# Moving one tile's transposes into the first tile's matmuls, and four weight splits to earlier page pairs, in a 2-layer decoder kernel

## The chip, the cores and the metric

The kernel is one program on one core of a Trainium2 chip. Its time is the device time of one execution in microseconds (us), and the number given for a kernel is the median of several executions. TensorE (PE in the profile) does the matmuls; VectorE (DVE), ScalarE (ACT) and GpSimd (POOL) do the rest of the arithmetic; SyncE (SP) issues every DMA. Each engine works through its own instructions in the order in which the program has them, and the engines meet only at semaphores: one engine waits until a counter that another one raises has reached a value.

## What is computed

Two layers of a decoder step on 512 prompt tokens and 8 sequences of 8 new tokens. Cut from the reference:

```python
def layer_forward(x, pos, p, ret_s0, ret_chunk, attend):
    h = rmsnorm(x, p['norm_w'])
    z = h @ p['w_in']                       # 1024 x 3264, all branches at once
    ...
    o_r, s_new = retention_scan(q_r, k_r, v_r, ret_s0.astype(jnp.float32), ret_chunk)
    ...
    o_a = attend(qn, qp, c, kpe, p).reshape(b, t, MLA_WIDTH) * jax.nn.silu(g_a)
    y = jnp.concatenate([o_r, o_a], axis=-1) @ p['w_out']   # 1024 x 1024
    return x + y, c, kpe, s_new.astype(x.dtype)
```

For the new tokens, `attend` reads 16 cached pages of 128 keys for each of the 8 sequences, projects the cached latents to keys, and attends over them.

## The kernel before, in words

Each layer L has three stages. **Stage 0** is the input projection. The tokens stand in five tiles t (four of 128 prompt rows, one of 64 sample rows). A tile is normed on DVE (`norm(t)`, L1588), turned by 8 transposes on PE (`x_turn(t)`, L593; 4 of them to a bank of PSUM, the memory that matmuls write), and kept as two parts, a high one by ACT (`keep_x_hi`, L1157) and a low one by DVE (`keep_x_lo`, L1574). A product of full precision is three matmuls: high by high, low weight by high, high weight by low (L562, L563, L564). The 3264 weight columns come in 8 groups g of 408; each group has four pieces `raw` of 2 chunks of the contraction each, split into `w_hi` (ACT, L1186) and `w_lo` (DVE, L1596). `tile_product(g, t)` is then 8 chunks c by 3 matmuls. In group 0 and tile 0 the products wait chunk by chunk for the weights (`w0`).

**Stage 1** is retention and the prompt's attention. **Stage 2** is decode, and then the output projection. Decode goes sequence by sequence, each in 8 pairs q of pages (`sequence`). For a pair, PE turns the next pair's latents (`turn_pair(n + 1)`, L954), then makes this pair's keys (`pair_keys`, 24 matmuls twice over one line, L977) and rotary scores (`pair_rotary`, L986). ACT keeps the turned latents (`keep_pair`, `cT_hi`, L1473, and `kpT`, L1476) and then squares this pair's keys (`square_pair`, L1486, L1489, L1491). DVE keeps the low part of the latents (`cT_lo`, L1983) and sums the squares (`sum_pair`, L2000). All three do the next pair's keeping ahead of this pair's squares and sums. The turned latents share one PSUM bank, so PE may only turn pair n + 1 once DVE has counted pair n's `cT_lo` (`c_lo_ok`).

Four pieces of the output weights (`wout0`, 344 columns) are loaded by SP at the beginning of stage 2 (L506), behind the 32 page loads of sequence 0 and ahead of those of sequence 1 (L490, L492). ACT and DVE split them into `w0_hi` (L1514) and `w0_lo` (L2064), one piece behind each of four pairs of the layer's first sequence. ACT's first piece waits for all four loads:

```python
                    if k == 0 and g == 0:
                        act.wait_ge(wout0_in, 16 * 4 * (L + 1))
```

The output projection, which reads them, comes after all eight sequences.

Of the kernel before, what the change touches and what calls it, by code (L numbers as in the profile page):

```python
# [39 lines left out]
DC = D // P  # L40
# [10 lines left out]
GW = COLS // NG  # L51
# [13 lines left out]
def rows(t):  # L65
    return ST if t == S_TILE else P
# [50 lines left out]
def build(nc, x_prompt, x_sample, cache_ckv, cache_kpe, state_ret, page_table, norm_w, w_in, q_a_norm_w,  # L117
# [57 lines left out]
    w_hi, w_lo = [], []  # L175
# [114 lines left out]
    ps = nc.alloc_psum_tensor("ps", [P, 8, 512], FP32)  # L290
# [4 lines left out]
    def sem(name, per_layer=True):  # L295
        s = nc.alloc_semaphore(name)
        if per_layer:
            layer_sems.append(s)
        return s
# [6 lines left out]
    BANK = (1, 2, 3, 4, 6)  # L306
# [6 lines left out]
    N_W = 4 * (NG + 3)  # L313
    N_RAW = NG + 1
    N_Y = 2 * TILES
    N_PAIR = NB * PAIRS
    W_PAR = (None, 1, 0)

    def mix_tile(k):
        return S_TILE if k == 0 else k - 1  # L320
# [14 lines left out]
    w_hi_ok, w_lo_ok, z_in_psum, z_kept = (sem(n) for n in  # L335
        ("w_hi_ready", "w_lo_ready", "z_in_psum", "z_kept"))
# [56 lines left out]
    def zc(t, c0, n):  # L393
        return z[0:rows(t), t, c0:c0 + n]
# [163 lines left out]
    def _(pe):  # L558
        def product(out, lhs, rhs, first, last):

            (a_hi, a_lo), (b_hi, b_lo) = lhs, rhs
            pe.matmul(out, a_hi, b_hi, start=first, stop=False)  # L562
            pe.matmul(out, a_hi, b_lo, start=False, stop=False)  # L563
            return pe.matmul(out, a_lo, b_hi, start=False, stop=last)  # L564

        def tile_products(out, t, w_h, w_l, chunks=range(DC), w0=None):

            for c in chunks:
                if w0 is not None and c % 2 == 0:
                    pe.wait_ge(w_lo_ok, w0 + c // 2 + 1)  # L570
                if t == S_TILE:
                    pe.matmul(out, hT_s[:, c, :], w_h(c), start=c == 0, stop=False)  # L572
                    m = pe.matmul(out, hT_s[:, c, :], w_l(c), start=False, stop=c == DC - 1)  # L573
                else:
                    rows_t = slice(t * P, (t + 1) * P)
                    m = product(out, (hT_hi[:, c, rows_t], hT_lo[:, c, rows_t]), (w_h(c), w_l(c)), c == 0, c == DC - 1)
            return m
# [3 lines left out]
        for L in range(DEPTH):  # L581

            def x_turn(t):

                n = rows(t)
                pe.wait_ge(x_normed, t + 1)
                for half in range(2):
                    u = 2 * t + half
                    if u >= 3:

                        pe.wait_ge(x_lo, u - 2)
                    for c in range(4):
                        m = pe.transpose(ps[:, X_BANKS[u % 3], c * P:c * P + n], zc(t, H0 + (4 * half + c) * P, P),  # L593
                                         ident[0:n, 0:n])
                    m.then_inc(x_turned, 1)

            def tile_product(g, t):
                if g == 0:
                    pe.wait_ge(x_lo, 2 * (t + 1))
                else:  # L600

                    pe.wait_ge(z_kept, (g - 1) * TILES + t + 1)
                w = (g + L) % 2
                tile_products(ps[:, BANK[t], 0:GW], t, lambda c: w_hi[w][:, c, :], lambda c: w_lo[w][:, c, :],
                              w0=N_W * L if g == 0 and t == 0 else None).then_inc(z_in_psum, 1)

            if L == 0:
                x_turn(0)
            x_turn(1)
            for t in range(TILES):  # L610
                if t >= 1 and t + 1 < TILES:
                    x_turn(t + 1)
# [455 lines left out]
            def out_chunks(g, t, chunks):  # L1068
# [3 lines left out]
                else:  # L1072
                    w_h, w_l = w_hi[W_PAR[g]], w_lo[W_PAR[g]]
                return tile_products(ps[:, BANK[t], 0:n_cols], t, lambda c: w_h[:, c, 0:n_cols],
# [75 lines left out]
    def _(act):  # L1150
# [11 lines left out]
        for L in range(DEPTH):  # L1162
# [303 lines left out]
            def keep_pair(n, q, first):  # L1466

                par = q % 2
                act.wait_ge(c_turned, n + 1)
                if not first:  # L1470

                    act.wait_ge(rp_ps, n - 1)
                act.activation(cT_hi[:, par, :, :].rearrange("p a n -> p (a n)"), ps[:, 0, :], ACT.Copy)\  # L1473
                    .then_inc(c_hi_ok, 1)
                act.wait_ge(kp_turned, n + 1)
                act.activation(kpT[:, par, :], ps[:, 5, 0:P], ACT.Copy).then_inc(kpT_ok, 1)  # L1476
# [17 lines left out]
            def tail_exp(s, b):  # L1494
                act.wait_ge(sh_ok, s + 1)
                act.activation(Pr[:, b, :, :], Ssc[:, b, :, :], ACT.Exp).then_inc(pr_ok, 1)

            def split_out(g, chunks=range(4)):
                n = OG[g + 1] - OG[g]
                for k in chunks:  # L1500
                    if k == 0 and g == 0:
                        act.wait_ge(wout0_in, 16 * 4 * (L + 1))
                    if k == 0 and g == 1:

                        act.wait_ge(wout1_in, 16 * 4 * (L + 1))
                        act.wait_ge(ds_ok, 2 * NB * (L + 1))
                    if g == 2:
                        if k == 0:

                            act.wait_ge(dy_ps, L + 1)  # L1510
                        act.wait_ge(raw_in[k], 16 * (N_RAW * L + NG + 1))
                    src = (wout0[:, k, :, :], wout1[:, k, :, :], raw[:, k, :, 0:n])[g]
                    dst = w0_hi if g == 0 else w_hi[W_PAR[g]]
                    act.activation(dst[:, 2 * k:2 * k + 2, 0:n], src, ACT.Copy).then_inc(w_hi_ok, 1)  # L1514
# [8 lines left out]
            def keep_y_hi(t):  # L1523
                keep_hi(t, Y_BANKS, y_turned, N_Y * L, y_hi, 0.5)

            def sequence(seq, b, first, last):
                for q in range(PAIRS):
                    n = seq * PAIRS + q
                    if q + 1 < PAIRS or not last:
                        keep_pair(n + 1, (q + 1) % PAIRS, first and q == 0)  # L1530
                    if q == 0 and not first:

                        act.wait_ge(ds_ok, seq * 2 - 1)
                    if last and q + 1 == PAIRS:
                        keep_y_hi(0)
                    square_pair(n, seq, b, q, first and q < 2)
                    if q == 3 and not first:
                        tail_exp(seq - 1, 1 - b)
                    if first and q >= 4:
                        split_out(0, (q - 4,))  # L1540

            keep_pair(S1 * PAIRS, 0, True)
            sequence(S1, 0, True, False)
# [20 lines left out]
    def _(dve):  # L1564
# [18 lines left out]
        for L in range(DEPTH):  # L1583
# [474 lines left out]
            def split_out(g, chunks=range(4)):  # L2058
                n = OG[g + 1] - OG[g]
                for k in chunks:  # L2060
                    dve.wait_ge(w_hi_ok, N_W * L + 4 * (NG + g) + k + 1)
                    src = (wout0[:, k, :, :], wout1[:, k, :, :], raw[:, k, :, 0:n])[g]
                    hi, lo = (w0_hi, w0_lo) if g == 0 else (w_hi[W_PAR[g]], w_lo[W_PAR[g]])
                    dve.tensor_tensor(lo[:, 2 * k:2 * k + 2, 0:n], src, hi[:, 2 * k:2 * k + 2, 0:n].bitcast(FP32),  # L2064
                                      ALU.subtract).then_inc(w_lo_ok, 1)

            def keep_y_lo(t):
                keep_lo(t, Y_BANKS, y_turned, y_hi, N_Y * L, y_lo, 0.5)
# [17 lines left out]
            def sequence(seq, b, first, last):  # L2086
                for q in range(PAIRS):
                    n = seq * PAIRS + q
                    if q + 1 < PAIRS or not last:
                        keep_pair(n + 1, (q + 1) % PAIRS, False)  # L2090
                    if not first:

                        if q == 2:
                            tail_diag(seq - 1)
                        if q == 3:
                            tail_shift(seq - 1, 1 - b)
                        if q == 6:
                            tail_divide(seq - 1)
                        if q == 7:
                            tail_keep(seq - 1)  # L2100
                    if q == 1 and not first:
                        half_scores(seq - 1, 1 - b, 1)
                        tail_max(seq - 1, 1 - b)
                    if first and q >= 4:
                        split_out(0, (q - 4,))
                    if last and q + 1 == PAIRS:
                        keep_y_lo(0)
                    sum_pair(n, b, q)
                    if q == 4:
                        half_scores(seq, b, 0)  # L2110
                        if not first:
                            tail_den(seq - 1, 1 - b)
                    if q == 5 and not last:
                        beside_w(seq + 1, 1 - b)
# [257 lines left out]
```

## Time and profile before

| | |
|---|---|
| median of 3 runs | 1260.67 us (1259.77 to 1263.28) |
| the profiled execution's own time | 1260.41 us |
| its span (first to last instruction) | 1258.6 us |
| PE busy | 1220.8 us, 97% of the span |
| DVE, ACT, POOL busy | 58%, 42%, 35% |
| mean granted clock of PE | 0.996 of full |

The span is 1.8 us below the execution's own time, which is the part of the time outside the first and last instruction; the own time is 0.3 us below the median. With PE at 97%, what matters is where PE is idle or its clock is low, and what PE waits for at those places.

### The profile page before, as it was taken

What the parts mean: (1) busy time and instruction counts of PE and PEld (TensorE: products, weight loads), DVE (VectorE), ACT (ScalarE), POOL (GpSimd) and SP (SyncE); (2) the same over time, 40 slices, a digit from 0 to 9 for tenths busy, and PEclk for the clock granted to TensorE, in tenths of its full rate; (3) what the DMA queues carried; (4) which work ended last, traced back from release to release, by engine and by line L of the source; (5) the groups of instructions that cost most, each with busy time, mean ns of one, the idle gap of its engine ahead of it and who ended that gap; (6) DMA issues with size and microseconds to landing.
All of it is one profiled execution on the core that took longest, in us unless ns stands there. A gap on an engine that the chain in (4) does not pass through costs nothing.

```text
span 1258.6 us, 26097 instructions
## 1 busy us (share of the span) xinstructions
PE 1220.8 (97%) x8624; PEld 1126.8 (90%) x8624; DVE 725.8 (58%) x1322; ACT 527.4 (42%) x1377; POOL 436.8 (35%) x632
## 2 busy tenths in 40 slices
PE   5999999998999999999999999999989999999998
PEld 4999995767999999999999999767779999999998
DVE  5445646665666666666463474556546666666652
ACT  4221324534655555553341122353446555555520
POOL 1014035441544454541011220554324544454400
PEclk9999999999999999999999999999999999999999
DMA  9331104102462232220743130320044433222021
GB/s 319 109 106 55 54 1 107 52 1 73 142 188 74 79 83 80 74 57 7 251 131 108 54 107 1 89 70 1 15 142 143 128 85 84 74 74 82 23 70 51
DMA packets 127906, 108.41 MB, mean 86 GB/s; under 512 B 45682, under 2 KB 123635, under 8 KB 127795
## 3 DMA queue, kind: packets, MB, share of 16 engines
q1 hardware_dynamic: 127794, 107.08, 28.4%
q8 instruction: 51, 0.84, 0.3%
q14 instruction: 61, 0.49, 0.1%
HBM read 96.12 MB, written 10.91 MB: 85 GB/s over the span
## 4 chain that ended last, share of the span: by engine, by line
PE 83%; issue 7%; DVE 3%; POOL 2%; ACT 2%; POOLq 1%; DVEq 1%; DMA 0%; ACTq 0%
PE ps L977 30%; PE ps L562 7%; PE ps L563 7%; PE ps L564 7%; PE ps L954 5%; PE ps L648 3%; PE ps L1006 3%; PE ps L572 2%; PE ps L573 2%; PE ps L986 2%; PE ps L804 1%; PE ps L827 1%; POOL rstat L2166 1%; PE ps L805 1%; PE ps L661 1%
## 5 line engine op out<-in xcount | busy, mean ns | idle before, releaser
L2000 DVE TENSOR_REDUCE kss<-ksq 128x8 f32<-128x1024 f32 x128 | 156.0, 1219 | 180.2 <-ACT ksq L1486 180.2
L562 PE MATMUL ps<-w_hi,hT_hi 128*128 128x408 f32 (+2 forms) x704 | 242.9, 345 | 0.0
L1486 ACT ACTIVATE ksq<-ps 128x544 f32<-128x544 f32 x256 | 159.9, 625 | 195.9 <-PE ps L977 195.3
L563 PE MATMUL ps<-w_lo,hT_hi 128*128 128x408 f32 (+2 forms) x704 | 239.9, 341 | 0.0
L564 PE MATMUL ps<-w_hi,hT_lo 128*128 128x408 f32 (+2 forms) x704 | 239.3, 340 | 0.0
L977 PE MATMUL ps<-wq_hi,cT_hi 128*128 128x272 f32 x1024 | 224.3, 300 | 0.0
L2336 POOL TENSOR_TENSOR krs<-kss_t,cst 128x8 f32<-128x8 f32 x128 | 209.2, 1634 | 19.0 <-issue 2.6
L977 PE MATMUL ps<-wq_lo,cT_hi 128*128 128x272 f32 x1024 | 212.4, 289 | 0.0
L977 PE MATMUL ps<-wq_hi,cT_lo 128*128 128x272 f32 x1024 | 212.4, 289 | 0.0
L977 PEld LDWEIGHTS ps<-wq_lo,cT_hi 128*128 128x128 f32 x1024 | 161.5, 189 | 0.0
L977 PEld LDWEIGHTS ps<-wq_hi,cT_lo 128*128 128x128 f32 x1024 | 161.3, 189 | 0.0
L977 PEld LDWEIGHTS ps<-wq_hi,cT_hi 128*128 128x128 f32 x1024 | 159.5, 190 | 0.0
L562 PEld LDWEIGHTS ps<-w_hi,hT_hi 128*128 128x128 f32 x704 | 132.8, 189 | 1.5 <-issue 1.2
L563 PEld LDWEIGHTS ps<-w_lo,hT_hi 128*128 128x128 f32 x704 | 132.9, 189 | 0.1
L564 PEld LDWEIGHTS ps<-w_hi,hT_lo 128*128 128x128 f32 x704 | 132.7, 188 | 0.2
L2329 POOL TENSOR_TENSOR kss_t<-kss,cst 128x8 f32<-128x8 f32 x128 | 27.4, 214 | 252.4 <-DVE kss L2000 252.4
L1192 ACT ACTIVATE z<-ps 64x408 f32<-64x408 f32 x16 | 8.1, 508 | 227.5 <-PE ps L573 227.5
L1473 ACT ACTIVATE cT_hi<-ps 128x512 fp32r<-128x512 f32 x128 | 77.9, 608 | 43.0 <-PE ps L954 42.9
L1983 DVE TENSOR_TENSOR cT_lo<-ps,cT_hi 128x512 fp32r<-128x512 f32 x128 | 87.5, 683 | 4.3 <-ACT cT_hi L1473 3.9
L954 PE MATMUL ps<-cst,ckv 128*128 128x128 f32 x512 | 79.8, 278 | 7.5 <-DVE cT_lo L1983 6.0
L2160 POOL TENSOR_SCALAR pool_tmp<-stat 128x1 f32<-128x1 f32 (+2 forms) x70 | 17.6, 252 | 197.2 <-ACTq L1170 79.9
L1612 DVE TENSOR_SCALAR z<-ps 128x408 f32<-128x408 f32 x64 | 35.3, 578 | 81.5 <-PE ps L564 80.6
(202 smaller groups left out, 1996.2 us busy)
## 6 DMA issues: line engine op xcount, KB each, us to landing
ckv<-in_cache_ckv SPq DMA_DIRECT2D x256, 128.0 KB, 2.0
raw<-in_w_in SPq DMA_DIRECT2D x64, 408.0 KB, 4.4
kp<-in_cache_kpe SPq DMA_DIRECT2D x256, 32.0 KB, 1.8
S<-in_state_ret SPq DMA_DIRECT2D x8, 512.0 KB, 6.0
out<-S SPq DMA_DIRECT2D x8, 512.0 KB, 3.2
wout<-in_w_out SPq DMA_DIRECT2D x8, 344.0 KB, 4.5
z<-in_w_out SPq DMA_DIRECT2D x8, 340.0 KB, 10.2
raw<-in_w_out SPq DMA_DIRECT2D x8, 340.0 KB, 4.5
```

The lines of the kernel that those rows point to most:

```text
L562: pe.matmul(out, a_hi, b_hi, start=first, stop=False)
L563: pe.matmul(out, a_hi, b_lo, start=False, stop=False)
L564: return pe.matmul(out, a_lo, b_hi, start=False, stop=last)
L648: m = pe.matmul(ps[0:n, half, 0:w], qlT[:, t % 2, c, 0:n], wqb[:, c, half * w:(half + 1) * w], start=c == 0, stop=c == QC - 1)
L954: m = pe.transpose(ps[:, 0, (2 * j + c) * P:(2 * j + c + 1) * P], ckv[b][:, 2 * q + j, c * P:(c + 1) * P], ident)
L977: m = pe.matmul(ps[:, 1 + 2 * j + side, 0:CUT], x, w[:, c, w0:w0 + CUT], start=c == 0 and k == 0, stop=c == KC - 1 and k == 2)
L1006: m = pe.matmul(ps[g * HQ:(g + 1) * HQ, 7, O_PV:O_PV + KVR], Pr[:, b, n, :], rhs, start=n < GROUPS, stop=n + GROUPS >= KT)
L1473: act.activation(cT_hi[:, par, :, :].rearrange("p a n -> p (a n)"), ps[:, 0, :], ACT.Copy)\
L1486: act.activation(ksq[:, q % 2, j, :].rearrange("p (s c) -> p s c", s=2), ps[:, 1 + 2 * j:3 + 2 * j, 0:CUT], ACT.Square).then_inc(kk_sq, 1)
L1983: dve.tensor_tensor(cT_lo[:, par, :, :].rearrange("p a n -> p (a n)"), ps[:, 0, :], cT_hi[:, par, :, :].rearrange("p a n -> p (a n)").bitc ...
L2000: dve.tensor_reduce(kss[:, hs, 2 * k:2 * k + 2, :], ksq[:, q % 2, :, c0:c0 + HW].rearrange("p j (h k) -> p j h k", h=H), AX.X, ALU.add).th ...
L2336: pool.tensor_tensor(krs[:, hs, c, :], tmp, spread_col(neg_half[:, 0:1]), ALU.pow)\
```

## The change

`x_turn(1)`, the transposes of tile 1, is issued in the middle of tile 0's group 0 products (behind chunk 3 of 8) and no longer ahead of them. No condition on the layer is in the code, so both layers get it. And in decode's first sequence of each layer the four weight pieces are split behind pairs 2, 3, 5 and 6 instead of 4, 5, 6 and 7, on ACT and on DVE.

```diff
+    W0_AT_PAIR = (2, 3, 5, 6)
...
-                tile_products(ps[:, BANK[t], 0:GW], t, lambda c: w_hi[w][:, c, :], lambda c: w_lo[w][:, c, :],
-                              w0=N_W * L if g == 0 and t == 0 else None).then_inc(z_in_psum, 1)
+                halves = (range(DC // 2), range(DC // 2, DC)) if g == 0 and t == 0 else (range(DC),)
+                for chunks in halves:
+                    if chunks[0]:
+                        x_turn(1)
+                    m = tile_products(ps[:, BANK[t], 0:GW], t, lambda c: w_hi[w][:, c, :], lambda c: w_lo[w][:, c, :],
+                                      chunks, w0=N_W * L if g == 0 and t == 0 else None)
+                m.then_inc(z_in_psum, 1)
...
             if L == 0:
                 x_turn(0)
-            x_turn(1)
...
-                    if first and q >= 4:
-                        split_out(0, (q - 4,))
+                    if first and q in W0_AT_PAIR:
+                        split_out(0, (W0_AT_PAIR.index(q),))
```

The last piece stands twice in the code, once in ACT's `sequence` and once in DVE's.

**PE at the program's start.** Before, the transposes of tiles 0 and 1 (L593, 16 in one row) stand ahead of the first tile's products:

```order
L593 MATMUL ps<-cst,z 128x128 x16
L562 MATMUL ps<-w_hi_72,hT_hi 128x408
L563 MATMUL ps<-w_lo_73,hT_hi 128x408
L564 MATMUL ps<-w_hi_72,hT_lo 128x408
L562 MATMUL ps<-w_hi_72,hT_hi 128x408
```

Now (line numbers are one higher) only tile 0's eight stand ahead, then 12 products, then tile 1's eight:

```order
L594 MATMUL ps<-cst,z 128x128 x8
L563 MATMUL ps<-w_hi_72,hT_hi 128x408
...
L565 MATMUL ps<-w_hi_72,hT_lo 128x408
L594 MATMUL ps<-cst,z 128x128 x8
L563 MATMUL ps<-w_hi_72,hT_hi 128x408
```

What moved are eight transposes, past 12 of the 24 products of tile 0.

**ACT in decode's first sequence, around the end of pair 2.** The rows are the last two of pair 2's squares, and then what stands behind them, before:

```order
L1489 ACTIVATE nope<-ps 128x32
L1491 ACTIVATE rot<-ps 128x64
L1473 ACTIVATE cT_hi<-ps 128x512
L1476 ACTIVATE kpT<-ps 128x128
L1486 ACTIVATE ksq<-ps 128x544
```

and now (line numbers five higher):

```order
L1494 ACTIVATE nope<-ps 128x32
L1496 ACTIVATE rot<-ps 128x64
L1519 ACTIVATE w_hi<-wout_78 128x688
L1478 ACTIVATE cT_hi<-ps 128x512
L1481 ACTIVATE kpT<-ps 128x128
L1491 ACTIVATE ksq<-ps 128x544
```

The first weight piece, with its wait for the four loads, now stands ahead of the keeping of pair 4's latents; it stood two pairs later.

**DVE in the same sequence.** Before, from the low part of pair 5's latents on, with a weight piece (L2064) behind it and behind pair 6's:

```order
L1983 TENSOR_TENSOR cT_lo<-ps,cT_hi 128x512
L2064 TENSOR_TENSOR w_lo<-wout_78,w_hi 128x688
L2000 TENSOR_REDUCE kss<-ksq 128x8
L2009 TENSOR_TENSOR Tn<-nope,krs 128x256
L2014 TENSOR_TENSOR Ssc<-rot,Tn 128x256
L1983 TENSOR_TENSOR cT_lo<-ps,cT_hi 128x512
L2064 TENSOR_TENSOR w_lo<-wout_78,w_hi 128x688
```

and now (line numbers five higher), from pair 4's latents on:

```order
L1988 TENSOR_TENSOR cT_lo<-ps,cT_hi 128x512
L2069 TENSOR_TENSOR w_lo<-wout_78,w_hi 128x688
L2005 TENSOR_REDUCE kss<-ksq 128x8
L1988 TENSOR_TENSOR cT_lo<-ps,cT_hi 128x512
L2005 TENSOR_REDUCE kss<-ksq 128x8
L2014 TENSOR_TENSOR Tn<-nope,krs 128x256
```

The slot with the half scores (`half_scores`, L2009 and L2014 before) has no weight piece any more; pairs 2 and 3 have one each.

## Rows read from the trace of the kernel before

**Rows 1.** Waits of PE over the whole span: us in total, times, longest.

```profile
PE ps L593 <- DVE z L1588: 15.2, 2, 9.6
PE ps L954 <- DVE cT_lo L1983: 6.0, 6, 1.4
```

**Rows 2.** Timeline, PE, start: start us, us, operation, idle before it and releaser.

```profile
17.17 1.97 PE L593 MATMUL ps<-cst,z 128*128 128x128 f32 x8 [5.60 <-DVE z L1588]
18.79 0.69 PE L562 MATMUL ps<-w_hi,hT_hi 128*128 128x408 f32 x1
19.27 0.54 PE L563 MATMUL ps<-w_lo,hT_hi 128*128 128x408 f32 x1
...
23.02 0.41 PE L562 MATMUL ps<-w_hi,hT_hi 128*128 128x408 f32 x1
...
25.31 1.03 PE L593 MATMUL ps<-cst,z 128*128 128x128 f32 x8
```

**Rows 3.** Timeline, DVE, start.

```profile
12.31 0.69 DVE L1574 SCALAR_TENSOR_TENSOR hT_lo<-ps,hT_hi 128x512 fp32r<-128x512 f32 x1 [0.15 <-ACT hT_hi L1157]
...
15.82 1.28 DVE L1588 SCALAR_TENSOR_TENSOR z<-z,rstat,norm_b 128x1024 f32<-128x1024 f32 x1 [0.89 <-POOL rstat L2166]
...
19.09 1.48 DVE L1574 SCALAR_TENSOR_TENSOR hT_lo<-ps,hT_hi 128x512 fp32r<-128x512 f32 x2
```

**Rows 4.** Timeline, ACT and DVE: group 1's weight split.

```profile
37.09 3.21 ACT L1186 ACTIVATE w_hi<-raw 128x816 fp32r<-128x816 f32 x4
...
38.01 3.76 DVE L1596 TENSOR_TENSOR w_lo<-raw,w_hi 128x816 fp32r<-128x816 f32 x4 [0.22 <-ACT w_hi L1186]
```

**Rows 5.** Timeline, PE, layer 1's `x_turn(1)`.

```profile
635.32 1.03 PE L593 MATMUL ps<-cst,z 128*128 128x128 f32 x8
```

**Rows 6.** Tile wout on SP: third and fourth load, layer 0, then layer 1.

```profile
L506 SPq DMA_DIRECT2D wout<-in_w_out x2: 469/469/469, 319.5 to 320.0; - x2
DMA to landing us min/median/max: 4.6/5.3/5.9
...
L506 SPq DMA_DIRECT2D wout<-in_w_out x2: 469/469/469, 935.6 to 936.1; - x2
DMA to landing us min/median/max: 4.8/5.4/6.0
```

**Rows 7.** Timeline, ACT, layer 0: behind pair 2, and weight pieces behind pairs 4, 6.

```profile
318.96 0.62 ACT L1473 ACTIVATE cT_hi<-ps 128x512 fp32r<-128x512 f32 x1
...
326.44 0.79 ACT L1514 ACTIVATE w_hi<-wout 128x688 fp32r<-128x688 f32 x1
...
335.45 0.79 ACT L1514 ACTIVATE w_hi<-wout 128x688 fp32r<-128x688 f32 x1
```

**Rows 8.** Timeline, DVE, layer 0: pair 4's sum, and a cast behind pair 5's.

```profile
328.06 1.21 DVE L2000 TENSOR_REDUCE kss<-ksq 128x8 f32<-128x1024 f32 x1
...
332.92 0.18 DVE L1991 CAST wq_hi<-qt_hi 128x64 fp32r<-128x64 f32 x1
```

**Rows 9.** Timeline, PE: turns of pairs 5 to 9 (layer 0), of pair 5 (layer 1).

```profile
321.97 0.61 PE L954 MATMUL ps<-cst,ckv 128*128 128x128 f32 x4
...
325.71 0.61 PE L954 MATMUL ps<-cst,ckv 128*128 128x128 f32 x4
...
330.94 0.66 PE L954 MATMUL ps<-cst,ckv 128*128 128x128 f32 x4 [1.33 <-DVE cT_lo L1983]
...
334.71 0.61 PE L954 MATMUL ps<-cst,ckv 128*128 128x128 f32 x4
...
338.93 0.66 PE L954 MATMUL ps<-cst,ckv 128*128 128x128 f32 x4 [0.32 <-DVE cT_lo L1983]
...
940.07 0.61 PE L954 MATMUL ps<-cst,ckv 128*128 128x128 f32 x4
```

**Rows 10.** Windows, layer 1: PE, PEld, DVE, ACT, POOL busy us, clock, DMA, GB/s.

```profile
918.00:924.00 6.00, 3.22 (x25) 2.56 (x25) 2.70 (x13) 1.41 (x4) 0.00 (x0) 1.00 0.33 93
924.00:928.00 4.00, 4.00 (x22) 4.00 (x21) 0.69 (x1) 1.48 (x4) 0.00 (x0) 0.57 0.38 108
```

More of the change, by code:

```diff
@@ L2103, in sequence @@
                         tail_max(seq - 1, 1 - b)
-                    if first and q >= 4:
-                        split_out(0, (q - 4,))
+                    if first and q in W0_AT_PAIR:
+                        split_out(0, (W0_AT_PAIR.index(q),))
                     if last and q + 1 == PAIRS:
```

## The prediction, made before the changed kernel ran

> **What bounds the kernel now.** I read the list of PE's waits first, since PE is busy for 97% of the span: any gain has to come out of PE's idle or slow time, and any loss must put idle time into PE. The list has two entries that the change touches [rows 1]. PE's transposes L593 waited 15.2 us in two places for DVE's norms, 9.6 of them at the very start; the other 5.6 us is the wait of `x_turn(1)`. And PE's page turns L954 waited 6.0 us in six places for DVE's `cT_lo`. The timelines at these places then give the terms. At the start PE stands idle until 17.17 us, when tile 1's norm is done, although tile 0 was complete long before: its last low part ended at 12.31 + 0.69 = 13.0 [rows 2, 3]. In decode's first sequence PE turns a pair every 3.74 us where nothing holds it (321.97 to 325.71), but takes 5.23 us to the turn of pair 7 (1.49 lost) and 4.22 us to that of pair 9 (0.48 lost), both waiting for `cT_lo` [rows 9]. These are the slots behind the first and the third weight piece, so the splits cost some 2.0 us of PE in each layer now.
>
> **Edit 1, layer 0: the gain.** The first product can start at 13.0 plus the 0.07 us that the chain takes from norm's end (15.82 + 1.28 = 17.10) to PE's start at 17.17, so at 13.1. PE's products run 0.341 us apart at first (11 steps from 19.27 to 23.02) and 0.191 apart later (12 steps from 23.02 to 25.31) [rows 2]; with 0.48 for the first, 12 of them end at 17.3. That is 0.15 us behind the norm, so the transposes of tile 1 start at 17.3 and take 1.62 us as now (17.17 to 18.79): 18.9. Twelve products are left. The slow spacing lasted 5.85 us from PE's restart (17.17 to 23.02). If it lasts as long from 13.1, it is over at 18.95 and the twelve take 2.3 us: tile 2's transposes start at 21.2 and no longer at 25.31, a gain of 4.1 us. Lower bound: the clock rises at the same time as now, 23.0; the twelve take 4.1 us and the gain is 2.3. Upper bound: it rises before the transposes, which then take about 0.8; the gain is 4.9. Tile 1's low part ends at 19.09 + 1.48 = 20.6, about 0.15 later now, ahead of its first product at 22 [rows 3]. Is the gain kept? What follows in stage 0 hangs on PE: group 1's weights were split by 37.09 + 3.21 on ACT and 38.01 + 3.76 = 41.8 on DVE, behind PE's transposes of tile 4; that work moves forward with PE [rows 4]. I take 4.1.
>
> **Edit 1, layer 1: nothing.** `x_turn(1)` at 635.32 has no wait in its row, and products stand directly behind it; PE does the same work in another order [rows 5]. Its cover is that tile 1's low part, 2.3 us later, is wanted only after all of tile 0.
>
> **Edit 2: the loss.** ACT was done with pair 2 and went to pair 4's latents at 318.96 [rows 7]. The first weight piece now stands there, and it waits for all four loads. SP issues the last at 320.0, and it lands 5.9 us later: 325.9. In layer 1 it is 936.1 + 6.0 = 942.1 [rows 6]. Today's first split at 326.44 comes right after that landing [rows 7]. Nothing in the change moves SP: the loads stand behind 32 page loads. So ACT stands still for 7 us, and what is queued behind it is `cT_hi` of pair 4, pair 3's squares and all the rest; DVE's `cT_lo` of pair 4 waits for it, and PE may not turn pair 5 without it. PE finishes pair 3's keys, which need nothing more, and stops. The way back I read from the slot of pair 6: ACT's piece at 335.45, PE's turn at 338.93, so 3.48 us for piece, DVE's piece, sum, `cT_lo` and the step to PE [rows 7, 9]. Pair 5's turn then comes at 325.9 + 3.5 = 329.4 instead of 321.97, 7.4 us late. In layer 1 it comes at 942.1 + 3.5 = 945.6 instead of 940.07, 5.5 us late; PE is there 1.9 us later against SP [rows 6, 9].
>
> What the other pieces do: behind pair 3 the piece finds DVE and ACT ahead of a PE that was stopped, no cost. Behind pair 4 there is none any more. DVE's sum began at 328.06 because it stood behind the piece [rows 8]; without it it begins some 1.6 us earlier, more than the 1.49 lost there, so that wait goes. Behind pair 5 a piece costs the ordinary 0.48, plus 0.2 for the two casts of the next sequence's queries (the first at 332.92, 0.18) that stand in the same slot [rows 8, 9]: 0.7. Behind pair 6 the piece is covered as pair 5's was (330.94 to 334.71 is 3.77). Layer 0: +7.4 -1.5 -0.5 +0.7 = +6.1. Layer 1: +5.5 -2.0 +0.7 = +4.2.
>
> **The clock.** PE now stands idle for about 7.3 and 5.4 us in the middle of decode. In layer 1 the granted clock fell at decode's start, after six microseconds in which PE was busy for only 3.22: it is 0.57 of full over 924 to 928 [rows 10]. With 0.5 as the low level (1.2 of 2.4 GHz) that is 0.43 x 4 / 0.5 = 3.4 us at it. At the program's start it was low for 5.85 us after PE's restart [rows 2]. Each low microsecond loses 1 - 0.191/0.341 = 0.44 us, so 1.5 to 2.6; I take 2.0 for each stall, 4.0 in all, with 0 and 5.2 as bounds. The Trainium skill (TensorE: Matmul & The Clock Gate, What's actually happening) says the same of the direction: "the default state is throttled, and activity releases the throttle". A reader who takes gaps of this size as free would get the sum without the 4.0.
>
> **A rule against the change.** The last of the four loads takes 5.9 and 6.0 us from issue to landing, behind three others in the same queue [rows 6]. The Trainium skill (DMA: Bandwidth & Descriptors, Rules for kernel authors) advises to issue a transfer early, compute, and wait on its semaphore late; this change waits earlier on a transfer that is issued no earlier. The same page's formula (Anatomy of one DMA: 2.0 us plus bytes over 436 GB/s) would give 2.8 us for one load of 344 KB against the 5.9 measured for the last of four; by it alone the last would land 3.1 us earlier and the sum would be about 6 us smaller. It prices one transfer on an empty queue, the row prices this one, and the row is used.
>
> **Sum.** -4.1 + 6.1 + 4.2 + 4.0 = +10.2 us, against the profiled execution's own time of 1260.4: 1270.6. That execution is 0.3 us below the median of 1260.7, so I say 1271.
>
> **Rivals.**
> - *The clock holds over both stalls.* For: single waits of up to 1.4 us, which PE has now, left it high at the turns of pairs 7 and 9, as the next turn's 3.77 us shows [rows 1, 9]. Against: in rows 10 six microseconds with PE idle for 2.8 of them were enough to lower it. Time: 1271 - 4 = 1267.
> - *The gain at the start is the small one.* The clock rises when it did before, 23.0. Time: 1271 + 1.8 = 1272.8. With the larger one, 1270.2.
> - *The landing is earlier than I read it.* If the last load lands about 3 us earlier in each layer (page loads of sequence 1 follow the weights and may be what stretches them), the stalls shrink by 6: 1265.
> - *The other side: faster.* One mechanism: the loads are complete when ACT comes to pair 2, so nothing waits. The first piece then costs the ordinary 0.5, the sum of edit 2 is -0.8 in each layer, and the time is 1260.7 - 4.1 - 1.6 = 1255. Its point of decision: with stalls of S in total, edit 2 is about S - 2.6, so the kernel is faster by over 3.8 us only if S is under 2.9 us, where rows 6 and 9 make it 12.9. The landing would have to be 5 us earlier in both layers. The rows speak against it: SP issues the third load only at 319.5, after ACT is there.
>
> **How the numbers follow.** Forecast 0.68; clock holds 0.11; small gain at the start 0.09; earlier landing 0.06; faster 0.04; something not named here 0.02. A measurement of this kernel tells 0.3%, 3.8 us, from no change. The first three are slower, and of the earlier landing all but a third. Low end: clock holds and gain 4.9 give 1266, the earlier landing 1265. High end: gain 2.3, clock 5.2 and half a microsecond more in each landing give 1275. Range 1265 to 1275.5. Slower by over 0.3%: 0.93; within: 0.03; faster: 0.04.
>
> **What the changed profile would show.** Products L563 from 13.1, transposes at 17.3, tile 2's at about 21.2. In decode's first sequence an idle time of PE of some 7 us (layer 0) and 5 to 6 us (layer 1) ahead of L954, released by DVE's `cT_lo`, while ACT's first weight piece is released by the DMA of wout; a granted clock of 0.5 for some microseconds behind each; no wait at pair 7's turn, 0.5 us at pair 8's. PE's waits for `cT_lo` go from 6.0 to some 17 us. I am wrong if ACT's first piece does not wait for the DMA, or if page loads of later sequences, started by PE, come to wait too.

## The result, and the profile after

| | before | after |
|---|---|---|
| median | 1260.26 us (1259.77 to 1263.28, 4 runs) | 1270.87 us (1269.77 to 1272.04, 4 runs) |
| profiled execution's own time, span | 1260.41, 1258.6 us | 1272.04, 1270.2 us |
| mean granted clock of PE | 0.996 | 0.989 |

The kernel before has one more execution here than in the table of the section on its time, so its median is a little lower. The ratio is 1.0076 (95% interval 1.0061 to 1.0091): the change costs 10.6 us. Below, a term is always read from the two profiled executions, which are 11.6 us apart.

The waits of PE over the whole span, after, to be read against [rows 1] (us in total, times, longest):

```profile
PE ps L959 <- DVE cT_lo L1988: 17.5, 6, 8.4
PE ps L594 <- DVE z L1593: 9.4, 1, 9.4
...
PE ps L563 <- DVE hT_lo L1579: 1.5, 1, 1.5
```

The 5.6 us ahead of `x_turn(1)` are gone and 1.5 us ahead of the first product have come; the wait for `cT_lo` is nearly three times what it was (17.5 against 6.0). The timeline of PE at the start answers to [rows 2] (start us, us, operation, idle before it and releaser):

```profile
12.85 0.71 PE L563 MATMUL ps<-w_hi,hT_hi 128*128 128x408 f32 x1 [1.48 <-DVE hT_lo L1579]
13.35 0.54 PE L564 MATMUL ps<-w_lo,hT_hi 128*128 128x408 f32 x1
13.69 0.54 PE L565 MATMUL ps<-w_hi,hT_lo 128*128 128x408 f32 x1
...
17.09 1.27 PE L594 MATMUL ps<-cst,z 128*128 128x128 f32 x8
18.12 0.43 PE L563 MATMUL ps<-w_hi,hT_hi 128*128 128x408 f32 x1
...
20.43 1.03 PE L594 MATMUL ps<-cst,z 128*128 128x128 f32 x8
```

Tile 2's transposes start at 20.43 instead of 25.31, 4.88 us earlier. The clock rose during tile 1's transposes: the next product stands 1.03 us behind their start, where it stood 1.62 behind before. This is read from the spacing of the products (0.341 us apart, then 0.19). The profile's granted clock does not show it: its windows print 1.00 at the start in both kernels, before (17 to 23 us) and after (12.85 to 17 us), although the products there are 0.341 apart.

In decode's first sequence, PE's turns of pairs 5 to 9 in layer 0 and of pairs 5 and 6 in layer 1 answer to [rows 9]:

```profile
326.77 1.11 PE L959 MATMUL ps<-cst,ckv 128*128 128x128 f32 x4 [8.36 <-DVE cT_lo L1988]
332.73 0.61 PE L959 MATMUL ps<-cst,ckv 128*128 128x128 f32 x4
336.46 0.61 PE L959 MATMUL ps<-cst,ckv 128*128 128x128 f32 x4
340.97 0.63 PE L959 MATMUL ps<-cst,ckv 128*128 128x128 f32 x4 [0.61 <-DVE cT_lo L1988]
344.72 0.61 PE L959 MATMUL ps<-cst,ckv 128*128 128x128 f32 x4
...
950.17 1.12 PE L959 MATMUL ps<-cst,ckv 128*128 128x128 f32 x4 [5.21 <-DVE cT_lo L1988]
956.68 0.60 PE L959 MATMUL ps<-cst,ckv 128*128 128x128 f32 x4
```

The turn ahead of 326.77 is at 314.50, so with 3.74 us for a period pair 5's was due at 318.24 and is 8.53 us late. In layer 1 the one before is at 941.06, the due time 944.80, and it is 5.37 us late. ACT and DVE in layer 0 show what was waited for, beside [rows 7, 8]:

```profile
323.30 0.78 ACT L1519 ACTIVATE w_hi<-wout 128x688 fp32r<-128x688 f32 x1 [7.94 <-DMA wout<-in_w_out]
323.99 0.58 ACT L1478 ACTIVATE cT_hi<-ps 128x512 fp32r<-128x512 f32 x1
...
324.11 0.88 DVE L2069 TENSOR_TENSOR w_lo<-wout,w_hi 128x688 fp32r<-128x688 f32 x1 [10.84 <-ACT w_hi L1519]
324.90 1.21 DVE L2005 TENSOR_REDUCE kss<-ksq 128x8 f32<-128x1024 f32 x1
326.03 0.68 DVE L1988 TENSOR_TENSOR cT_lo<-ps,cT_hi 128x512 fp32r<-128x512 f32 x1
```

One chain: ACT waits 7.94 us for the DMA, DVE for ACT, PE for DVE. From ACT's piece to PE's turn it is 3.47 us. ACT's first piece in layer 1:

```profile
946.71 0.78 ACT L1519 ACTIVATE w_hi<-wout 128x688 fp32r<-128x688 f32 x1 [4.79 <-DMA wout<-in_w_out]
```

From there it is 3.46 us to the turn at 950.17. What SP's loads of `wout` show, layer 0 and then layer 1, beside [rows 6] (here over all four loads of a layer, of which the last is the longest):

```profile
L507 SPq DMA_DIRECT2D wout<-in_w_out x4: 389/469/471, 315.4 to 316.8; - x4
DMA to landing us min/median/max: 3.6/4.4/6.5
...
L507 SPq DMA_DIRECT2D wout<-in_w_out x4: 390/469/472, 939.3 to 940.8; - x4
DMA to landing us min/median/max: 3.0/4.2/5.9
```

The last lands at 316.8 + 6.5 = 323.3 and 940.8 + 5.9 = 946.7, the moments at which ACT starts its first piece. The windows around the stall in layer 0, and one behind the stall in layer 1 (PE, PEld, DVE, ACT, POOL busy us, granted clock, DMA share, GB/s), where [rows 10] had shown such a drop at the start of decode:

```profile
321.00:327.00 6.00, 0.23 (x1) 0.23 (x2) 2.86 (x4) 3.41 (x9) 0.52 (x3) 0.53 0.44 121
327.00:331.60 4.60, 4.60 (x22) 4.60 (x22) 2.35 (x3) 1.45 (x4) 4.12 (x4) 0.50 0.52 143
331.60:336.00 4.40, 4.40 (x38) 4.40 (x38) 2.42 (x4) 2.23 (x8) 1.00 (x3) 1.00 0.32 85
...
950.00:957.00 7.00, 6.83 (x34) 6.83 (x35) 2.72 (x4) 1.88 (x6) 4.38 (x5) 0.56 0.33 94
```

In layer 0 PE comes back at the low one of its two levels, 1.2 GHz, and works at it until about 331.6, for 4.8 us: 22 rows of matmuls in the last 4.6 us of it, then 38 in 4.4. In layer 1 the 0.56 over the 7 us from 950.00 comes to 0.44 x 7 / 0.5 = 6.2 us at the low level. So the period behind the stall is 5.96 us (326.77 to 332.73) instead of 3.74, and in layer 1 it is 6.51 (950.17 to 956.68).

### The profile page after: what moved, and what is told of

It reads as the page before. It is cut to its first block, busy times and chain, and to the rows that moved or that the text cites. A ratio compares the mean times of both kernels' runs of the same rounds, so it can differ in the third digit from the quotient of the medians.

```text
span 1270.2 us, 26097 instructions
## 1 busy us (share of the span) xinstructions
PE 1225.1 (96%) x8624; PEld 1130.5 (89%) x8624; DVE 725.6 (57%) x1322; ACT 527.3 (42%) x1377; POOL 438.8 (35%) x632
## 4 chain that ended last, share of the span: by engine, by line
PE 79%; issue 7%; SPq 4%; DVE 3%; POOL 2%; DMA 2%; ACT 1%; POOLq 1%; DVEq 1%; ACTq 0%
PE ps L982 28%; PE ps L563 7%; PE ps L564 7%; PE ps L565 7%; PE ps L959 4%; PE ps L653 3%; PE ps L1011 3%; PE ps L573 2%; PE ps L574 2%; PE ps L991 2%; POOL rstat L2171 1%; PE ps L809 1%; PE ps L666 1%; SPq L491 1%; SPq L477 1%
## 5 line engine op out<-in xcount | busy, mean ns | idle before, releaser
L959 PE MATMUL ps<-cst,ckv 128*128 128x128 f32 x512 | 80.7, 281 | 19.0 <-DVE cT_lo L1988 17.5
L959 PEld LDWEIGHTS ps<-cst,ckv 128*128 128x128 f32 x512 | 61.5, 156 | 26.1 <-DVE cT_lo L1988 17.1
```

What stands on the lines that cost most here:

```text
L959: m = pe.transpose(ps[:, 0, (2 * j + c) * P:(2 * j + c + 1) * P], ckv[b][:, 2 * q + j, c * P:(c + 1) * P], ident)
```

## The experiments

A ratio is always to the kernel before on the same chip. Its medians are 1261.13 us (experiments 1, 2, 3 and the first try of 7), 1261.22 (4, 5, 6 and 8) and 1261.39 (9 and the second try of 7).

**1. The first edit alone.**

```diff
-    W0_AT_PAIR = (2, 3, 5, 6)
+    W0_AT_PAIR = (4, 5, 6, 7)
```

> Only the first edit (the second tile's transposes inside the first tile's products); the weight pieces stay behind pairs 4 to 7. If the two edits are independent, as the prediction's sum has it: 4 to 5 us faster than before, 1255.5, with PE's tile 2 transposes at about 20.4 and PE's waits for cT_lo still 6.0 us in all. If the gain at the start is eaten later (group 1's weights or a constant arriving at a fixed time), the same time as before.

Measured: 1255.89 us (1254.67 to 1256.67), ratio 0.9959 (0.9945 to 0.9972), 5.2 us faster. Tile 2's transposes are at 20.66. PE's waits for `cT_lo` are as before, 6.0 us in 6 places.

**2. The second edit alone** (`x_turn(1)` ahead of the products as before, pieces behind pairs 2, 3, 5, 6).

> Only the second edit (pieces behind pairs 2, 3, 5, 6). Theory 'landing': both stalls of 8 and 5 us and the low clock behind them, some 15 us slower than before, 1275. Theory 'the edits are coupled' (the stalls come from the first edit moving PE ahead of SP's loads): the stalls shrink or vanish without the first edit, within 5 us of before.

Measured: 1276.63 us (1275.41 to 1277.43), ratio 1.012 (1.0104 to 1.0135), 15.5 us slower. The two edits add up: -5.2 + 15.5 = +10.3, against 10.6 for both. Its turns of pair 5, layer 0 and layer 1, are 7.9 and 5.9 us late, so the stalls do not come from the first edit:

```profile
330.64 1.12 PE L955 MATMUL ps<-cst,ckv 128*128 128x128 f32 x4 [7.72 <-DVE cT_lo L1984]
...
955.76 1.12 PE L955 MATMUL ps<-cst,ckv 128*128 128x128 f32 x4 [5.74 <-DVE cT_lo L1984]
```

**3. No landing to wait for** (both edits; the pieces are read from a part of `z` that is long complete, so the output projection multiplies by other numbers; the loads are still issued). Besides the lines shown, SP waits for DVE's last piece before it loads the old x into `z`. That holds nothing up: DVE starts this piece at 333.44 us in layer 0, and SP comes to the old x, behind its page loads, at 349.30.

```diff
-                    if k == 0 and g == 0:
-                        act.wait_ge(wout0_in, 16 * 4 * (L + 1))
...
-                    src = (wout0[:, k, :, :], wout1[:, k, :, :], raw[:, k, :, 0:n])[g]
+                    src = (z[:, k, 0:2 * n].rearrange("p (c n) -> p c n", c=2), wout1[:, k, :, :], raw[:, k, :, 0:n])[g]
```

> Both edits, but the four pieces are read from columns of z that have long been there, and ACT does not wait for the loads (the output projection then uses wrong weights; the loads are still issued). Theory 'landing': no stall at pair 5's turn, no low clock behind it, one wait of 0.5 to 0.8 us behind pair 2 and one behind pair 5 in each layer: 1254. Theory 'early slots have no room' (the loss comes from the pieces' own work behind pairs 2 and 3, not from the loads): it stays near 1271.

Measured: 1257.33 us (1253.84 to 1258.34), ratio 0.9963 (0.9949 to 0.9976). Same instructions in the same early slots, 13.5 us less than the changed kernel, though 3.3 above the expected 1254. Its longest waits of PE for `cT_lo` (L960) and for pages:

```profile
PE ps L960 <- DVE cT_lo L1987: 4.6, 6, 1.4
...
PE ps L960 <- DMA ckv<-in_cache_ckv: 1.7, 2, 0.9
```

The slots as such are 1.4 us better than the old ones in this wait (4.6 against 6.0), about the 0.8 per layer that the prediction's last rival gave them; but 1.7 us come back in a new wait for pages, and against experiment 1 nothing is won. The profiled execution, the slowest of the five, also lost the clock at decode's start in both layers, where that of experiment 1 lost it in one.

**4. A semaphore for each load.** The four loads raise one each, and ACT's piece waits for its own alone.

```diff
-                    if k == 0 and g == 0:
-                        act.wait_ge(wout0_in, 16 * 4 * (L + 1))
+                    if g == 0:
+                        act.wait_ge(wout0_in[k], 16 * (L + 1))
```

> Both edits, the pieces behind pairs 2, 3, 5 and 6, but each of the four loads raises a semaphore of its own and ACT's piece waits for its own load alone. Landing theory (the loss is the time from ACT's coming to the piece to the landing it waits for): now the first load's landing decides, issued at about 318.6 in layer 0 and 938.0 in layer 1 by the clock of before, and landing 3.0 to 3.6 us later. ACT is there at 319.0, so PE's turn of pair 5 comes about 3 us late in layer 0 and about 1.5 us late in layer 1, no or little low clock behind it, and PE's waits for cT_lo fall from 32 to some 8 us. Time: about 1258, 13 us below the changed kernel and 3 below the one before. Rival (the early slots are themselves too full for a piece, whatever it waits for): PE's waits stay near those of the changed kernel, and the time near 1271.

Measured: 1260.89 us (1256.83 to 1264.29, 12 runs), ratio 0.9994 (0.9982 to 1.0007), no difference from the kernel before that can be told. PE's turns of pairs 5 and 6, in layer 0 and layer 1:

```profile
321.69 0.66 PE L960 MATMUL ps<-cst,ckv 128*128 128x128 f32 x4 [1.96 <-DVE cT_lo L1989]
325.47 0.61 PE L960 MATMUL ps<-cst,ckv 128*128 128x128 f32 x4
...
940.22 0.66 PE L960 MATMUL ps<-cst,ckv 128*128 128x128 f32 x4 [2.52 <-DVE cT_lo L1989]
944.01 0.61 PE L960 MATMUL ps<-cst,ckv 128*128 128x128 f32 x4
```

Due at 319.57 and 937.53, they are 2.1 and 2.7 us late, in sum 4.8. The expected 3 and 1.5 have nearly the same sum, but each layer's was off. PE's waits for `cT_lo` are 8.4 us. (Two figures of the expectation are slips: the changed kernel has 17.5 us of these waits, not 32, and SP issues the first load of layer 1 at 934.64 before, not at 938.0.) So the rival falls: of the 15.5 us that the second edit costs alone, some 10 went with the wait for the three later loads, the low clock behind it included. The 4.8 us that are left are the wait for the first load. Behind both stops the next period is 3.78 and 3.79 us, so the clock held. The median is 3 us above the expected 1258; the profiled execution took 1259.34.

**5. The first piece one pair later.**

```diff
-    W0_AT_PAIR = (2, 3, 5, 6)
+    W0_AT_PAIR = (3, 5, 6, 7)
```

> Both edits, but only the first weight piece one pair later: behind pairs 3, 5, 6 and 7. Landing theory: ACT comes to the wait 3.74 us later while the landing stays where it is, so the stalls of 8.5 and 5.4 us become 4.8 and 1.7, and the low clock behind them shrinks or goes: 5.0 less. Time: 1271 less 7.4 less 3 to 5, so 1258.5 to 1260.5. If the length of the stall did not hang on the place but on the piece being first (a fixed cost of the wait), the time would stay at 1271.

Measured: 1263.64 us (1258.71 to 1267.56, 11 runs), ratio 1.0022 (1.0009 to 1.0035): 7 us better than the changed kernel, 3 above what was expected. In the profiled execution (1261.57 us), from the turn of pair 1 on:

```profile
303.05 0.81 PE L959 MATMUL ps<-cst,ckv 128*128 128x128 f32 x4 [1.36 <-DVE cT_lo L1988]
308.36 0.61 PE L959 MATMUL ps<-cst,ckv 128*128 128x128 f32 x4
...
325.33 0.63 PE L959 MATMUL ps<-cst,ckv 128*128 128x128 f32 x4 [1.86 <-DVE cT_lo L1988]
329.08 0.61 PE L959 MATMUL ps<-cst,ckv 128*128 128x128 f32 x4
...
943.93 0.63 PE L959 MATMUL ps<-cst,ckv 128*128 128x128 f32 x4 [2.18 <-DVE cT_lo L1988]
949.21 0.61 PE L959 MATMUL ps<-cst,ckv 128*128 128x128 f32 x4
```

The turns of pair 6 are 2.0 and 2.3 us late, where 4.8 and 1.7 were expected. In layer 0 the last load landed 1.3 us earlier against PE's turn of pair 1 than in the changed kernel, and PE came 1.5 us later, since its clock fell at decode's start (303.05 to 308.36 is 5.31 us, and 3.78 in the changed kernel). Behind the first stall the next period is 3.75 us, behind the second 5.28: there the clock fell, and stayed low for 3.4 us. Experiments 4 and 5 have stalls of this size, and their executions lie 7.5 and 8.9 us apart, where those of the kernel before lie 4.5 apart on the same chip. That the landing and the clock differ from one execution to the next would explain both the spread and the 3 us, but only one execution of each has a trace.

**6. Work in place of idleness.** The changed kernel, with extra matmuls on PE ahead of the turn that is late; nobody uses their result.

```diff
+                    if first and q == 4:
+                        for _ in range(36 if L else 60):
+                            pe.matmul(ps[:, 7, 0:272], cT_hi[:, 1, 0, :], wq_hi[:, 0, 0:272], start=True, stop=True)
```

> The changed kernel, and ahead of the turn that waits for the late cT_lo in each layer's first sequence PE does extra matmuls whose result nobody uses (60 of 272 columns in layer 0, 36 in layer 1, into a PSUM bank that is free there), so that PE is busy for most of each stall and stands still no longer than before. Clock theory (the stalls cost more than their length, because PE comes back at 0.5 of its clock): turns of pair 5 as late as in the changed kernel, but the next period is 3.74 and no longer 5.96 and 6.51 us, so the time falls by up to 5.0 us, to about 1266. Rival (the slower next period is the engines behind PE, catching up, and not the clock): same time as the changed kernel, 1271.

Measured: 1267.78 us (1266.68 to 1268.0), ratio 1.0047 (1.0034 to 1.006), 3.1 us less than the changed kernel though PE does more (4.3 us less between the two profiled executions). Pair 5's turn and the next, in layer 0 and layer 1:

```profile
326.08 0.60 PE L959 MATMUL ps<-cst,ckv 128*128 128x128 f32 x4
329.80 0.61 PE L959 MATMUL ps<-cst,ckv 128*128 128x128 f32 x4
...
948.51 0.66 PE L959 MATMUL ps<-cst,ckv 128*128 128x128 f32 x4 [2.43 <-DVE cT_lo L1991]
952.30 0.61 PE L959 MATMUL ps<-cst,ckv 128*128 128x128 f32 x4
```

The periods behind the stalls are 3.72 and 3.79 us, where the changed kernel has 5.96 and 6.51: the slow period was the clock, 5.0 us in all (the granted clock is 1.00 from 326 to 330 and from 948.5 to 952.3). Layer 1 shows it best, where PE still waits 2.43 us for `cT_lo`. In layer 0 the extra work was too long: PE's turn has no idle time in its row and comes 5.1 us behind ACT's piece (at 320.97), not 3.5, so that the other engines had time to catch up as well. Of the 5.0 us 0.7 go back, since the turns come 0.5 and 0.2 us later, counted from decode's first matmul; that leaves the 4.3.

**7. ACT's and DVE's pieces one slot apart.** The first edit, ACT's pieces behind pairs 4, 5, 6, 6 and DVE's behind 5, 6, 7, 7, so that DVE's sum no longer stands behind a piece that has just been made.

```diff
-    W0_AT_PAIR = (2, 3, 5, 6)
+    W0_ACT, W0_DVE = (4, 5, 6, 6), (5, 6, 7, 7)
```

> The first edit, and the pieces placed so that DVE never waits for ACT's: ACT behind pairs 4, 5, 6, 6, DVE's low parts in the slots of pairs 5, 6, 7, 7, which is ahead of that pair's sum, where DVE is idle for 1.9 us. If the old waits at pairs 7 and 9 come from DVE's piece standing ahead of its sum and behind ACT's, they go: 4 us less than the first edit alone, 1251.5. If it is ACT's work that holds PE there, the waits stay and the time is that of the first edit alone, 1255.5, or more, since ACT now has two pieces behind pair 6.

Measured: 1256.33 us (1254.31 to 1259.21), ratio 0.9966 (0.9952 to 0.998). The waits at the pieces are gone (`cT_lo` 2.7 us in all, the list before had 6.0), and yet the median is no better than experiment 1's and 4.8 us above the expected 1251.5. A second try, on the chip of experiment 9:

> The lagged pieces once more (1256.3 before, on another chip), beside the next kernel. If moving SP's other loads was worth only the waits for the DMA of ckv and not a difference between chips, this comes out at 1254 to 1256; if the chips differ, at 1252 to 1253.

Measured: 1257.0 us (1253.8 to 1258.1, 6 runs), ratio 0.9956 (0.9942 to 0.9971), above what was expected (1254 to 1256), and not the 1252 to 1253 of chips that differ. The profiled one is the slowest of the six (1258.1 us). Its list of waits and a turn in the second sequence show what had come in place of the old waits:

```profile
PE ps L959 <- DMA ckv<-in_cache_ckv: 3.6, 2, 2.1
...
PE ps L959 <- DVE cT_lo L1988: 2.7, 2, 1.4
```

```profile
365.07 0.72 PE L959 MATMUL ps<-cst,ckv 128*128 128x128 f32 x4 [2.09 <-DMA ckv<-in_cache_ckv]
370.38 0.61 PE L959 MATMUL ps<-cst,ckv 128*128 128x128 f32 x4
```

PE now waits for the pages of sequence 2, which SP issues behind its loads of the old x and of four other weight pieces, and after 2.1 us of it the clock fell once more (5.31 us to the next turn). In the first try the same wait was 0.7 us in one place.

**8. SP's other loads behind all page loads**, in the kernel of experiment 7 (the `Fori` over the page loads stands ahead of the loads of the old x and of `wout1`).

> The kernel with the first edit and the pieces lagged by one pair between ACT and DVE (1256.3), and beside that SP's loads of the old x and of the other output weights moved behind all page loads. Theory (once PE no longer waits for cT_lo it comes to wait for the pages of sequence 2, 0.7 to 0.9 us in each layer, since SP issues them behind these other loads): the waits of PE for the DMA of ckv go, and the time falls by about 1 to 1.5 us, to about 1255. Rival (SP is not what holds the pages back, but the buffers of sequence 0 coming free): the waits stay and so does the time, 1256.3.

Measured: 1251.07 us (1251.0 to 1253.29), ratio 0.9925 (0.9912 to 0.9938): the fastest kernel here, 10.2 us under the one before. No wait for `ckv` is left in its list. It is 5.3 and 5.9 us faster than the two tries of experiment 7 (5.2 and 3.9 by the ratios, since the chips differ), where I had expected 1 to 1.5: I had priced the wait at profiles in which it was short. The other profile's 3.6 us, and 1.5 us for one drop of the clock behind it, make 5. This pricing rests on one traced execution of each kernel; that moving the loads is what helps rests on all executions, of which the slowest here (1253.29) is faster than the fastest of experiment 7 (1253.8).

**9. SP's loads moved, pieces at their old places.**

> The first edit, the weight pieces behind pairs 4, 5, 6 and 7 as before, and SP's loads of the old x and of the other output weights behind all page loads. If what SP has ahead of the pages of sequence 2 matters only once PE no longer waits for cT_lo, nothing changes against the first edit alone: 1255.9. If both causes add up independently (2.7 us for the lag, about 1.1 for SP's order), it is 1254 to 1255. If SP's order was worth all of the 5 us between the lagged kernels, it is about 1251.

Measured: 1256.14 us (1255.93 to 1258.0), ratio 0.996 (0.9947 to 0.9974), the same as experiment 1. So SP's order is worth nothing while PE is late for `cT_lo`, and the lag is worth nothing in the median while SP is late with the pages; together they are worth 4 to 5 us. The waits at pairs 7 and 9, which the lag takes away, are 3.9 us of that.

## Why the prediction was right

The forecast was 1271.0 us and the time is 1270.87. Its steps, one by one, with sizes from the two profiled executions:

| step | predicted | measured |
|---|---|---|
| first edit, layer 0 | -4.1 | -4.88 |
| first edit, layer 1 | 0 | 0 |
| stall at pair 5's turn, layer 0, layer 1 | +7.4, +5.5 | +8.53, +5.37 |
| old waits at pairs 7 and 9, both layers | -4.0 | -3.94 |
| new wait at pair 8, both layers | +1.4 | +1.54 |
| clock behind the stalls | +4.0 | +2.22 +2.77 |
| sum | +10.2 | +11.6 |

The terms measured sum to 11.61, and the executions' own times differ by 11.63.

- *The gain at the start* came out at the upper bound (4.9) and not at the 4.1 taken. PE's first product came at 12.85 instead of 13.1, since everything in this execution began 0.25 us earlier (20.66 for tile 2 in experiment 1), and the rest is the clock, which rose within the transposes; I had let the slow spacing last 5.85 us again, and it lasted about 5 (in experiment 8 it ended already among the first twelve products). The gain was kept to the end of stage 0. In layer 1 the turn stands inside the products without a wait, and the stretch from the end of decode in layer 0 to stage 1 in layer 1 takes 213.83 us before and 213.86 after.
- *The stalls.* The mechanism is as predicted, link by link, and the way back of 3.48 us measures 3.47 and 3.46. Layer 0 is 1.1 us longer because SP issued 0.5 us later against PE and the last load took 6.5 us, not 5.9. Experiment 3 shows that the stalls are the wait for the landings, but for the ordinary 0.5 us of a piece in each layer, and experiment 4 that all but 4.8 of the 13.9 us are the wait for the last three. The last landing took between 5.0 and 7.4 us in the profiles of the experiments; what stretches it was not tested.
- *The clock* was mis-sized by 1.0: I took two microseconds, in the middle of 1.5 to 2.6, and the stalls cost 2.22 and 2.77, the second above the bound of 2.6. What was short is the time at the low level: 4.8 and about 6 us after PE's restart, where I had seen 3.4 and 5.85. The 5.85, which I called a low clock, was read from the spacing of the products, not from a granted clock. Experiment 6 shows that this is the clock and not the other engines catching up; the rival that the clock holds over both stalls falls.
- *The rule against the change*: the Trainium skill (DMA: Bandwidth & Descriptors, Rules for kernel authors) advises to wait late on a transfer issued early. Experiments 3 and 4 agree: the same slots without the wait for a landing cost no more than the old ones (4.6 us of PE's waits against 6.0), and a wait for one load instead of four costs 4.8 us instead of 13.9. The 2.8 us for one such load, an estimate from the same page's formula (Anatomy of one DMA), comes near the shortest of the four at best (3.6 and 3.0 us measured), not the last (6.5 and 5.9); the page fitted that formula to transfers issued by GpSimd, and these are issued by SP.

The mechanism was right, but the hit to 0.1 us is in part luck. The profiled terms sum to 11.6 and not to 10.2: the gain was taken 0.8 too small, stall and clock 1.0 each too small. The profiled execution is the slowest of the four, and the medians lie only 10.6 apart.

## What to carry to other kernels

Before work is moved to an earlier slot of an engine, look up when its data land and what stands behind it on that engine: here a wait of 8 us on ACT, an engine that is busy 42% of the time, stopped PE through DVE, and a semaphore shared by four loads made the first piece wait for the last. A stall of PE costs more than its length, by 1.5 to 2.8 us here, if the clock falls with it. And where two causes are late at nearly the same time, taking away either one showed nothing here (experiments 7 and 9): look at what is next in the list of waits, and take away both.

## What the runs showed of the hardware

The granted clock of PE also falls where no long stall stands, at the beginning of stage 1 (PE idle for 2.1 to 2.4 us) and of decode (1.4 us). The program has these stretches in every execution, but the clock falls in some of the profiled ones and not in others. At the beginning of stage 1 in layer 0 the kernel before kept full clock and the changed one did not, with no instruction moved there (the window before, and then the one after):

```profile
192.00:196.00 4.00, 3.56 (x20) 2.67 (x21) 3.60 (x5) 3.49 (x7) 3.17 (x4) 1.00 0.71 194
```

```profile
188.00:192.00 4.00, 4.00 (x14) 2.76 (x13) 3.67 (x4) 3.43 (x7) 2.51 (x3) 0.57 0.95 249
```

In layer 1 it was the other way round, so that the two nearly cancel (+1.1 and -1.0 us in stage 1). The beginning of decode does the same, in layer 0 or layer 1 or both. Each such drop costs 1.0 to 1.5 us. That this is much of what executions of one kernel differ by is likely, but not shown, since only one of each has a trace.

The length of a stop alone does not tell whether the clock falls. At the beginning of stage 1 the idle time is 2.14 us in layer 0 and 2.33 in layer 1 before, 2.16 and 2.36 after, and the clock fell in layer 1 before and in layer 0 after. Elsewhere it held over stops of PE of 1.86 us (experiment 5, layer 0), 1.96 and 2.52 (experiment 4) and 2.43 (experiment 6, layer 1), and it fell with stops of 2.09 (experiment 7, second try) and 2.18 us (experiment 5, layer 1), and with the four of 5.2 us and more.
